# Activation written in turn order, and down weights dealt to partitions to match, in a one-core mixture-of-experts layer

## The chip, the cores and the metric

The kernel runs on one core of one Trainium2 chip. The metric is the device time in microseconds. Before the change it is 1559.59 us, the median of 3 runs (1559.12 to 1560.1).

## The reference, cut to what matters

One layer of a streaming encoder: 512 tokens of width 1024 go through a token mixer (RWKV heads, pooling, forgetting attention), and then through a mixture of 32 experts, of which each token takes its top 4. The change touches only the experts:

```python
def expert_block(args):
    x_blk, e = args                       # 128 tokens of one expert, 1024 wide
    gu = x_blk @ w_gu[e] + b_gu[e]        # w_gu[e]: 1024 x 2048
    gate = jnp.minimum(gu[:, :D_FF], SWIGLU_LIMIT)
    up = jnp.clip(gu[:, D_FF:], -SWIGLU_LIMIT, SWIGLU_LIMIT)
    act = (up + 1.0) * (gate * jax.nn.sigmoid(SWIGLU_ALPHA * gate))
    return act @ w_down[e] + b_down[e]    # w_down[e]: 1024 x 1024, the sum runs over the 1024 columns of act
```

The sum over the columns of `act` may be taken in any order, as long as column f of `act` meets row f of `w_down`.

## The kernel before, in words

**Stages.** The first 320 us or so are the mixer, then come router and output projection, and from about 382 us to 1526 us the experts. One step handles one expert with one block of 128 tokens; there are 32 steps of the same shape, and a few microseconds of combining after them.

**Weights.** Each expert's weights arrive as 12 chunks of 1 MB (128 partitions x 2048 f32): 8 of gate and up (`c < KT`), 4 of down. Each chunk is loaded by SyncE into one of 8 raw slots (`load`, L1602 to L1613), once TensorE has used the chunk 8 before. ScalarE copies it into the rounded form `w_hi` (`split_hi`, L1619; 4 slots, so it waits until TensorE has used the chunk 4 before). VectorE subtracts, `w_lo = w_raw - w_hi` (`split_lo`, L1625), in the raw slot's own place. TensorE multiplies in three parts, 12 matmuls of 512 columns a chunk (`chunk`, L2330), and counts the chunk as used.

**Down chunks before.** Down chunk j holds the rows 256 j to 256 j + 255 of the expert's down weights, two to a partition: partition p has the rows 256 j + 2p and 256 j + 2p + 1. That is 8 KB in one run for a partition, and 1 MB in one run for the chunk.

**The activation.** TensorE leaves gate in PSUM banks 0 and 1 and up (with 1 added by the bias) in banks 2 and 3, as 128 tokens x 1024 columns each. ScalarE writes the sigmoid into `sig_b` (L1776). VectorE makes the product in `act_b` by three instructions in `swiglu(n)`: L2055 (up, clipped, from PSUM), L2058 (times the capped sigmoid, from SBUF), L2061 (times the capped gate, from PSUM). Here all of them read and write columns in their own order, next to each other.

**The turns.** `at_turn(n)` (L2342 to L2348) transposes the activation on TensorE, 128 columns at a time, 8 transposes (L2346) with `act_b` as the operand that is loaded into the array. Turn k = 2j + i takes the columns 256 j + i, + 2, + 4 and so on, so every second column. The transposes of the tokens (`xt`, L2309) have the same shape but read 128 columns next to each other. ScalarE and VectorE split the turned activation into `aTh` (L1763) and `aTl` (L2066, `a_lo`), the tokens into `xTh` and `xTl` (`x_lo`).

**Order on VectorE in step n** (function `step`): `swiglu(n-1)`, `x_lo(n)`, the 8 `split_lo` of gate and up of expert n, `a_lo(n-1)` , the 4 `split_lo` of down of expert n-1. All of it is in program order.

**Order on TensorE in step n**: wait for `swiglu(n-1)`; bias (L2319, 4 matmuls into banks 0 to 3); wait for `xTl`; gate and up chunks 0 to 3; `at_turn(n-1)`; chunks 4 to 7; `xt(n+1)`; the 4 down chunks of expert n-1. Each chunk waits for its `w_lo`.

**Order on ScalarE in step n**: sigmoid of n-1, `xTh`, four `w_hi`, the store of a finished output block, four `w_hi`, `aTh`, four `w_hi`.

In step 1 the `w_lo` of chunk 0 is made before `swiglu(0)` (`EARLY = 1`); in the steps 2 to 31 it is made after `swiglu` and `x_lo`.

Of the kernel before, what the change touches and what calls it, by code (L numbers as in the profile page):

```python
# [20 lines left out]
ALU = mybir.AluOpType  # L21
# [3 lines left out]
P = 128  # L25
D = 1024
S = 512
KT = D // P
# [19 lines left out]
F = 1024  # L48
# [8 lines left out]
CHUNKS = 12  # L57
# [9 lines left out]
LIMIT, ALPHA = 7.0, 1.702  # L67
# [72 lines left out]
def build(nc, a, out):  # L140
    with ExitStack() as ctx:
        def sb(name, shape, dt=F32):
            return ctx.enter_context(nc.sbuf_tensor(name, shape, dt))

        def sem(name):
            return ctx.enter_context(nc.semaphore(name))
# [13 lines left out]
        def Rc(lo, hi):  # L160
            if hi <= LATE:
                return R0[:, lo:hi]
            if hi <= FV_LO:
                return R1[:, lo - LATE:hi - LATE]
            if hi <= FV_HI:
                return R2[:, lo - FV_LO:hi - FV_LO]
            return R1[:, lo - LATE - PZ_LO + FV_LO:hi - LATE - PZ_LO + FV_LO]
        ident = sb("ident", [P, P])
# [30 lines left out]
        sat = sb("sat", [P, 1])  # L199
# [129 lines left out]
        ps = ctx.enter_context(nc.psum_tensor("ps", [P, 8, 512], F32))  # L329
# [104 lines left out]
        up_rdy = sem("up_rdy")  # L434
        half_rdy = sem("half_rdy")
# [11 lines left out]
        act_rdy = sem("act_rdy")  # L447
# [1098 lines left out]
        sig_b, act_b = Rc(11264, 12288), Rc(12288, 13312)  # L1546
# [17 lines left out]
        dn_v = a["moe_w_down"][0].rearrange("e k n -> (e k) n")  # L1564
# [14 lines left out]
        def wait_used(eng, at, back=0):  # L1579

            if len(at) == 3:
                eng.wait_ge(w_used, CHUNKS * at[1] + (CHUNKS * E + at[2] + 1 - back))
            else:
                eng.wait_ge(w_used, 2 * CHUNKS * at[0] + (at[1] + 1 - back))
# [17 lines left out]
        def load(sp, e, c, at, first=False):  # L1602

            if len(at) == 3:
                wait_used(sp, at, 4 if c < RAW_SLOTS else RAW_SLOTS)
            elif not first:
                wait_used(sp, at, RAW_SLOTS)
            s = at[-1] % RAW_SLOTS
            if c < KT:
                src = gu_v[bass.ds(e * D + P * c, P), :]  # L1610
            else:
                src = dn_v[bass.ds(e * F + 2 * P * (c - KT), 2 * P), :].rearrange("(p i) n -> p (i n)", i=2)
            sp.dma_start(w_raw[:, s, :], src).then_inc(raw_in[s], 16)  # L1613

        def split_hi(act, at, first=False):
# [17 lines left out]
        @block.sync  # L1633
        def _(sp):
            sp.wait_ge(rw_out, 2)
            for c in range(KT):
                if c == 2:
                    sp.wait_ge(p_mm, TT)
                load(sp, 0, c, place(0, c), first=True)
            for part in range(3):  # L1640
                sp.dma_start(bdn_all[E * part:E * part + E, :], a["moe_b_down"][0]).then_inc(bdn_in, 16)
            for c in range(CHUNKS):
                load(sp, 1 if c < KT else 0, c, place(1, c))
            sp.wait_ge(ov_rdy, 1)
            sp.dma_start(normfB, a["norm_f"].partition_broadcast(P)).then_inc(normf_in, 16)
            with sp.Fori(1, E // 2) as m:
                for s in range(2):
                    for c in range(CHUNKS):
                        load(sp, 2 * m + s if c < KT else 2 * m + (s - 1), c, lap(m, s, c))
            for c in range(KT, CHUNKS):  # L1650
                load(sp, E - 1, c, place(E, c - KT))
            ov = overflow_count(sp)
            with sp.If(ov > 0):
                sp.wait_ge(flushed, 1)
                with sp.Fori(0, ov) as j:
                    e = sp.value_load(ovI[0:1, bass.ds(j, 1)], min_val=0, max_val=E - 1)
                    for c in range(CHUNKS):
                        load(sp, e, c, extra(j, c))
            for t in range(TT):
                sp.wait_ge(res_rdy, t + 1)  # L1660
                sp.dma_start(out[0, P * t:P * t + P, :], x2[:, t, :]).then_inc(out_done[t % 2], 16)
# [203 lines left out]
        def _(dve):  # L1865
# [14 lines left out]
            v = nc.vector  # L1880

            def two(buf):
                return buf.rearrange("p (b c) -> p b c", b=2)


            dve.wait_ge(small2_in, 16 * SMALL2)
            v.tensor_scalar(braw[HD:P, :, :], braw[HD:P, :, :], 1.0, None, ALU.add).then_inc(bias_one, 1)
# [4 lines left out]
                                   op0=ALU.mult, op1=ALU.add).then_inc(bias_lo, 1)  # L1892
            dve.wait_ge(mod_dma, 16 * 14)
            link(v.scalar_tensor_tensor(out=mod[4], in0=mod[4], scalar=1.0, in1=norm2B,
                                        op0=ALU.add, op1=ALU.mult))
# [61 lines left out]
            for t in range(TT):  # L1957
# [9 lines left out]
                if t == 0:  # L1967
                    mixed_lo(4)
                    for m in (4, 5):
# [6 lines left out]
                                            op0=ALU.mult, op1=ALU.mult))  # L1976
# [75 lines left out]

            def swiglu(n, gu_end):
                wait_used(dve, gu_end)
                v.tensor_scalar(two(act_b), ps[:, 2:4, :], 1.0 - LIMIT, 1.0 + LIMIT, ALU.max, ALU.min).then_inc(up_rdy, 1)  # L2055
                dve.wait_ge(sig_rdy, n + 1)
                dve.wait_ge(up_rdy, n + 1)
                v.scalar_tensor_tensor(out=act_b, in0=sig_b, scalar=sat[:, 0:1], in1=act_b, op0=ALU.min,  # L2058
                                       op1=ALU.mult).then_inc(half_rdy, 1)
                dve.wait_ge(half_rdy, n + 1)  # L2060
                v.scalar_tensor_tensor(out=two(act_b), in0=ps[:, 0:2, :], scalar=LIMIT, in1=two(act_b), op0=ALU.min,  # L2061
                                       op1=ALU.mult).then_inc(act_rdy, 1)

            def turned_lo(n, ev_sem, hi_part, lo_part, lo_sem):
                dve.wait_ge(ev_sem, n + 1)
# [52 lines left out]
            def step(n, where, before, done=0, side=0):  # L2118
                swiglu(n - 1, before(KT - 1))
                x_lo(n)  # L2120
                for c in range(KT):
                    if c >= done:
                        split_lo(dve, where(c))
                    beside(side, c)
                a_lo(n - 1)
                for c in range(KT, CHUNKS):
                    split_lo(dve, where(c))
# [31 lines left out]
            with dve.Fori((TT + 2) // 2, E // 2) as m:  # L2159
                for s in range(2):  # L2160
                    step(2 * m + s, lambda c: lap(m, s, c), lambda c: lap(m, s, c - CHUNKS))
            swiglu(E - 1, place(E - 1, KT - 1))
            split_lo(dve, place(E, 0))
            rows_here(0)
# [11 lines left out]
            with dve.If(ov > 0):  # L2176
                for t in range(1, TT - 1):
                    into_x(t, link_over)
                dve.wait_ge(yg_in[TT - 1], 16 * TOPK)
                link_over(v.tensor_scalar(yg[TT - 1][0], yg[TT - 1][0], gate_of[:, 0, TT - 1, 0:1], None, ALU.mult))  # L2180
                for k in range(1, TOPK):
                    link_over(add_row(TT - 1, 0, k))
                into_x(TT - 1, link_over).then_inc(flushed, 1)
                with dve.Fori(0, ov) as j:
                    x_lo(E + j)
                    for c in range(KT):
                        split_lo(dve, extra(j, c))
                    swiglu(E + j, extra(j, KT - 1))
                    a_lo(E + j)
                    for c in range(KT, CHUNKS):  # L2190
                        split_lo(dve, extra(j, c))

                dve.wait_ge(over_in, 16 * TT * TOPK)
                tail_diag(1, tail_new)
                for t in range(TT - 1):
                    link_over(v.tensor_scalar(yg[t][0], yg[t][0], gate_of[:, 1, t, 0:1], None, ALU.mult))
                    for k in range(1, TOPK):
                        link_over(add_row(t, 1, k))
                link_over(into_x(0, link_over))
# [26 lines left out]
        def _(pe):  # L2226
# [115 lines left out]
            def at_turn(n):  # L2342
                pe.wait_ge(act_rdy, n + 1)
                for k in range(KT):
                    j, i = k // 2, k % 2
                    ins = nc.tensor.transpose(ps[:, 4 + k // 4, P * (k % 4):P * (k % 4) + P],  # L2346
                                              act_b[:, 2 * P * j + i:2 * P * (j + 1):2], ident[:])
                ins.then_inc(at_mm, 1)  # L2348

            def bias_down(t, start):  # L2350
# [68 lines left out]
            step(E - 1, 1, at_step(E - 1), None, E - 2, 1, True)  # L2419
            pe.wait_ge(gmt_rdy, 2)  # L2420
            at_turn(E - 1)
            pe.wait_ge(y_last, 1)
            tail_add(0, 0, True, False)
# [8 lines left out]
            with pe.If(ov > 0):  # L2432
# [3 lines left out]
                with pe.Fori(0, ov) as j:  # L2436
                    n = E + j
# [52 lines left out]
```

## Time and profile before

| | us |
|---|---|
| median of 3 runs | 1559.59 (1559.12 to 1560.1) |
| the profiled execution's own time | 1562.78 |
| its span (first to last instruction) | 1561.0 |
| TensorE busy in the span | 1503.5 |
| VectorE busy | 1375.4 |
| ScalarE busy | 1006.5 |
| GpSimd busy | 225.2 |

The granted TensorE clock is 0.986 of full speed over the span. DMA moves 507.71 MB, 325 GB/s over the span. A matmul's duration in the profile (about 0.39 us for 512 columns) is longer than the distance to the next (about 0.227 us), because matmuls are pipelined; how long work on TensorE takes is read from the distance of starts. "PEld" is the loading of the array, which runs beside the matmuls.

### The profile page before, as it was taken

The page shows a single profiled execution, that of the slowest core. Times are in us where ns is not written, and L with a number is a line of the kernel's source. Part 1 is how long each engine was busy: PE and PEld are TensorE (multiplying, and loading weights), DVE is VectorE, ACT ScalarE, POOL GpSimd, SP SyncE. Part 2 cuts the span into 40 slices and gives each one's busy share as a digit, 9 for nine tenths or more (in the row PEclk, how much of TensorE's full clock was granted, in tenths as well). Part 3 has the DMA queues.
Part 4 walks back from the last instruction along what each step waited for, and adds up shares of the span by engine and source line. Part 5 has one row for each costly group of instructions (what it writes and reads, how often), then busy time and mean ns, then how long its engine had stood idle before and what let it go on. Part 6 is the DMA issues. An engine that isn't in the chain of part 4 may idle for free.

```text
span 1561.0 us, 22569 instructions
## 1 busy us (share of the span) xinstructions
PE 1503.5 (96%) x8449; PEld 1177.0 (75%) x8449; DVE 1375.4 (88%) x1068; ACT 1006.5 (64%) x820; POOL 225.2 (14%) x236
## 2 busy tenths in 40 slices
PE   4999989998899999999999999999999999999996
PEld 2684468666788888888888888888888888888873
DVE  6887577487999999999999999999999999999996
ACT  4332434344577777777777777777777777777762
POOL 3343031000011111111111111111111111110060
PEclk9999999997999999999999999999999999999998
DMA  9679130225899999999999999999999999999992
GB/s 362 259 263 348 58 115 26 73 82 226 299 384 383 390 388 386 379 393 393 395 380 395 384 393 377 384 397 382 384 399 389 381 385 391 384 385 376 378 357 108
DMA packets 89544, 507.71 MB, mean 325 GB/s; under 512 B 11384, under 2 KB 12712, under 8 KB 38160
## 3 DMA queue, kind: packets, MB, share of 16 engines
q1 hardware_dynamic: 74656, 454.65, 74.3%
q0 software_dynamic: 9104, 34.08, 6.3%
q10 hardware_dynamic: 5728, 18.18, 2.9%
q8 instruction: 40, 0.66, 0.2%
q14 instruction: 16, 0.13, 0.0%
HBM read 478.03 MB, written 28.85 MB: 325 GB/s over the span
## 4 chain that ended last, share of the span: by engine, by line
PE 90%; DVE 5%; DMA 2%; ACT 1%; issue 1%; POOL 0%; SPq 0%; DVEq 0%; POOLq 0%; ACTq 0%
PE ps L2330 67%; PE ps L2346 2%; PE ps L1369 2%; PE ps L2309 2%; PE ps L1441 2%; PE ps L1267 2%; PE ps L1355 2%; PE ps L1361 2%; PE ps L1358 2%; DMA Wt<-in_ada_w 1%; PE ps L1363 1%; PE ps L2387 1%; PE ps L2319 1%; PE ps L2236 1%; PE ps L1323 1%
## 5 line engine op out<-in xcount | busy, mean ns | idle before, releaser
L1625 DVE TENSOR_TENSOR w_lo<-w_raw,w_hi 128x2048 fp32r<-128x2048 f32 x384 | 865.2, 2287 | 62.9 <-ACT w_hi L1619 59.5
L1619 ACT ACTIVATE w_hi<-w_raw 128x2048 fp32r<-128x2048 f32 x384 | 736.2, 1919 | 273.2 <-PE ps L2330 273.2
L2330 PE MATMUL ps<-w_hi,xTh 128*128 128x512 f32 x1024 | 407.1, 398 | 2.5 <-DVE xTl L2066 2.2
L2330 PE MATMUL ps<-w_lo,xTh 128*128 128x512 f32 x1024 | 400.5, 391 | 0.0
L2330 PE MATMUL ps<-w_hi,xTl 128*128 128x512 f32 x1024 | 274.7, 390 | 0.0
L2330 PEld LDWEIGHTS ps<-w_hi,xTh 128*128 128x128 f32 x1024 | 193.4, 189 | 49.9 <-issue 7.5
L2330 PEld LDWEIGHTS ps<-w_hi,xTl 128*128 128x128 f32 x1024 | 192.8, 188 | 40.6
L2330 PEld LDWEIGHTS ps<-w_lo,xTh 128*128 128x128 f32 x1024 | 193.3, 189 | 38.1
L2330 PE MATMUL ps<-w_hi,aTh 128*128 128x512 f32 x512 | 202.4, 395 | 0.0
L2330 PE MATMUL ps<-w_lo,aTh 128*128 128x512 f32 x512 | 199.4, 389 | 0.0
L1667 POOL TENSOR_TENSOR carried<-iotaE 128x1 f32<-128x1 f32 x64 | 28.0, 438 | 992.4 <-PE ps L2309 869.7
L2330 PE MATMUL ps<-w_hi,aTl 128*128 128x512 f32 x512 | 157.6, 389 | 0.0
L2330 PEld LDWEIGHTS ps<-w_hi,aTl 128*128 128x128 f32 x512 | 96.1, 188 | 20.1
L2330 PEld LDWEIGHTS ps<-w_lo,aTh 128*128 128x128 f32 x512 | 96.3, 188 | 19.1 <-issue 0.2
L2330 PEld LDWEIGHTS ps<-w_hi,aTh 128*128 128x128 f32 x512 | 96.2, 188 | 19.0 <-issue 0.2
L1679 POOL DMA_INDIRECT xg<-h_rows,icol x30 | 86.4, 2880 | 4.4 <-issue 0.4
L802 ACT ACTIVATE R<-ps,fmx 128x128 f32<-128x128 f32 (+3 forms) x32 | 16.6, 523 | 46.0 <-DVE fmx L1031 46.0
L2058 DVE SCALAR_TENSOR_TENSOR R<-R,sat 128x1024 f32<-128x1024 f32 x32 | 41.1, 1284 | 3.8
L683 POOL TENSOR_TENSOR Wr<-Wt,Wr 128x1024 fp32r<-128x1024 f32 x13 | 35.0, 2695 | 64.7 <-ACT Wr L778 64.7
L2061 DVE SCALAR_TENSOR_TENSOR R<-ps,R 128x1024 f32<-128x1024 f32 x32 | 39.2, 1224 | 1.1
L2055 DVE TENSOR_SCALAR R<-ps 128x1024 f32<-128x1024 f32 x32 | 38.9, 1217 | 0.7 <-PE ps L2330 0.7
L2066 DVE TENSOR_TENSOR xTl<-ps,xTh 128x1024 fp32r<-128x1024 f32 x32 | 38.8, 1213 | 0.6 <-ACT xTh L1763 0.6
(425 smaller groups left out, 1577.1 us busy)
## 6 DMA issues: line engine op xcount, KB each, us to landing
w_raw<-in_moe_w_gu SPq DMA_DIRECT2D x256, 1024.0 KB, 6.9
w_raw<-in_moe_w_down SPq DMA_DIRECT2D x128, 1024.0 KB, 7.7
y_rows<-R ACTq DMA_DIRECT2D x30, 512.0 KB, 7.7
Wt<-in_ada_w SPq DMA_DIRECT2D x10, 1024.0 KB, 4.6
y_rows<-Wt POOLq DMA_DIRECT2D x1, 8704.0 KB, 24.6
Wt<-in_ada_w SPq DMA_DIRECT2D x16, 512.0 KB, 11.7
Wt<-in_w_in SPq DMA_DIRECT2D x4, 2048.0 KB, 9.6
R<-in_ada_w SPq DMA_DIRECT2D x6, 1024.0 KB, 8.2
```

The source lines that it names most:

```text
L683: g.tensor_tensor(blk_lo[at][:, :, c], blk[at][:, :, c], set_hi[i % 2].bitcast(F32), ALU.subtract).then_inc(set_rest, 1)
L1267: ins = mm(job_bank(("rw", m)), blk[0][:, k, P * m:P * m + P], hT[:, k, :], start=(k == 0), stop=(k == KT - 1))
L1355: mm(b, w_hi_[:, k, :], h_hi[:, k, :], start=(k == 0), stop=False)
L1358: mm(b, w_hi_[:, k, :], h_lo[k], start=False, stop=False)
L1619: nc.scalar.activation(w_hi[:, at[-1] % HI_SLOTS, :], w_raw[:, at[-1] % RAW_SLOTS, :], ACT.Copy).then_inc(hi_rdy, 1)
L1625: nc.vector.tensor_tensor(w_lo[:, s, :], w_raw[:, s, :], w_hi[:, at[-1] % HI_SLOTS, :].bitcast(F32), ALU.subtract).then_inc(lo_rdy, 1)
L1679: nc.gpsimd.indirect_dma_start(out=xg[s], out_offset=None, in_=h2_d, in_offset=bass.IndirectOffsetOnAxis(ap=ids, axis=0)).then_inc(xg_in[s ...
L2055: v.tensor_scalar(two(act_b), ps[:, 2:4, :], 1.0 - LIMIT, 1.0 + LIMIT, ALU.max, ALU.min).then_inc(up_rdy, 1)
L2058: v.scalar_tensor_tensor(out=act_b, in0=sig_b, scalar=sat[:, 0:1], in1=act_b, op0=ALU.min, op1=ALU.mult).then_inc(half_rdy, 1)
L2061: v.scalar_tensor_tensor(out=two(act_b), in0=ps[:, 0:2, :], scalar=LIMIT, in1=two(act_b), op0=ALU.min, op1=ALU.mult).then_inc(act_rdy, 1)
L2066: v.tensor_tensor(lo_part[:], ps[:, 4:6, :].rearrange("p b (k t) -> p (b k) t", k=4), hi_part[:].bitcast(F32), ALU.subtract).then_inc(lo_s ...
L2330: ins = mm(ps[:, bank0 + c, :], x[:, k, :], w[:, 512 * (banks * i + c):512 * (banks * i + c) + 512], start=(first and i == 0 and x is xh a ...
```

## The change: what it does

`act_b` is written in the order in which the turns read it: column f = 8 q + k of the product goes to place 128 k + q. `by_k` makes the view in which VectorE's three instructions read their sources: for each k it takes the columns k, k + 8, k + 16 and so on, so consecutive elements lie 8 f32 (32 bytes) apart. `act_k` is the destination and second source, whose elements lie next to each other. Turn k then reads 128 columns next to each other, and holds column 8 q + k in partition q.

To match, the down chunk j has in partition p the rows 8p + 2j and 8p + 2j + 1. A partition still reads 8 KB in one run, but the runs of neighbouring partitions lie 32 KB apart instead of 8 KB.

```diff
             else:
-                src = dn_v[bass.ds(e * F + 2 * P * (c - KT), 2 * P), :].rearrange("(p i) n -> p (i n)", i=2)
+                src = dn_v[bass.ds(e * F, F), :].rearrange("(p c i) n -> p c (i n)", c=CHUNKS - KT, i=2)[:, c - KT, :]
             sp.dma_start(w_raw[:, s, :], src).then_inc(raw_in[s], 16)
...
+            def by_k(banks):
+
+                return banks.rearrange("p b c -> p (b c)").rearrange("p (q k) -> p k q", k=KT)
+
+            act_k = act_b.rearrange("p (k q) -> p k q", k=KT)
...
             def swiglu(n, gu_end):
                 wait_used(dve, gu_end)
-                v.tensor_scalar(two(act_b), ps[:, 2:4, :], 1.0 - LIMIT, 1.0 + LIMIT, ALU.max, ALU.min).then_inc(up_rdy, 1)
+                v.tensor_scalar(act_k, by_k(ps[:, 2:4, :]), 1.0 - LIMIT, 1.0 + LIMIT, ALU.max, ALU.min).then_inc(up_rdy, 1)
                 dve.wait_ge(sig_rdy, n + 1)
                 dve.wait_ge(up_rdy, n + 1)
-                v.scalar_tensor_tensor(out=act_b, in0=sig_b, scalar=sat[:, 0:1], in1=act_b, op0=ALU.min,
-                                       op1=ALU.mult).then_inc(half_rdy, 1)
+                v.scalar_tensor_tensor(out=act_k, in0=by_k(two(sig_b)), scalar=sat[:, 0:1], in1=act_k,
+                                       op0=ALU.min, op1=ALU.mult).then_inc(half_rdy, 1)
                 dve.wait_ge(half_rdy, n + 1)
-                v.scalar_tensor_tensor(out=two(act_b), in0=ps[:, 0:2, :], scalar=LIMIT, in1=two(act_b), op0=ALU.min,
-                                       op1=ALU.mult).then_inc(act_rdy, 1)
+                v.scalar_tensor_tensor(out=act_k, in0=by_k(ps[:, 0:2, :]), scalar=LIMIT, in1=act_k,
+                                       op0=ALU.min, op1=ALU.mult).then_inc(act_rdy, 1)
...
                 for k in range(KT):
-                    j, i = k // 2, k % 2
                     ins = nc.tensor.transpose(ps[:, 4 + k // 4, P * (k % 4):P * (k % 4) + P],
-                                              act_b[:, 2 * P * j + i:2 * P * (j + 1):2], ident[:])
+                                              act_b[:, P * k:P * k + P], ident[:])
                 ins.then_inc(at_mm, 1)
```

## Rows read from the trace of the kernel before

**Rows 1.** The page: busy time by engine.

```profile
PE 1503.5 (96%) x8449; PEld 1177.0 (75%) x8449; DVE 1375.4 (88%) x1068; ACT 1006.5 (64%) x820; POOL 225.2 (14%) x236
```

**Rows 2.** The page: lines in the chain that ended last, share of span.

```profile
PE ps L2330 67%; PE ps L2346 2%; PE ps L1369 2%; PE ps L2309 2%; PE ps L1441 2%; PE ps L1267 2%; PE ps L1355 2%; PE ps L1361 2%; PE ps L1358 2%; DMA Wt<-in_ada_w 1%; PE ps L1363 1%; PE ps L2387 1%; PE ps L2319 1%; PE ps L2236 1%; PE ps L1323 1%
```

**Rows 3.** Waits, whole span: engine, line, waited for: us total, times, longest.

```profile
ACT w_hi L1619 <- PE ps L2330: 273.2, 343, 6.0
DVE w_lo L1625 <- ACT w_hi L1619: 59.5, 150, 0.5
```

**Rows 4.** Windows, one step: length, busy by engine, PEclk, DMA share, GB/s.

```profile
600.00:635.18 35.18, 35.18 (x166) 28.94 (x165) 32.87 (x18) 26.68 (x18) 3.95 (x4) 1.00 0.99 389
```

**Rows 5.** Timeline, VectorE, one step: start us, us, instruction.

```profile
1009.10 1.22 DVE L2055 TENSOR_SCALAR R<-ps 128x1024 f32<-128x1024 f32 x1
1010.44 1.28 DVE L2058 SCALAR_TENSOR_TENSOR R<-R,sat 128x1024 f32<-128x1024 f32 x1
...
1014.03 15.73 DVE L1625 TENSOR_TENSOR w_lo<-w_raw,w_hi 128x2048 fp32r<-128x2048 f32 x7
```

**Rows 6.** Timeline, TensorE, the same step: start us, us, instruction.

```profile
1003.83 1.07 PE L2330 MATMUL ps<-w_hi,xTl 128*128 128x512 f32 x4
...
1005.53 0.48 PE L2330 MATMUL ps<-w_hi,aTh 128*128 128x512 f32 x1
...
1017.03 0.51 PE L2330 MATMUL ps<-w_hi,xTh 128*128 128x512 f32 x1
...
1019.87 0.39 PE L2330 MATMUL ps<-w_hi,xTh 128*128 128x512 f32 x1
...
1027.12 1.08 PE L2330 MATMUL ps<-w_hi,xTl 128*128 128x512 f32 x4
...
1028.91 0.48 PE L2330 MATMUL ps<-w_hi,xTh 128*128 128x512 f32 x1
```

**Rows 7.** Groups by form, array loads of the turns: busy us, mean ns, idle.

```profile
L2346 PEld LDWEIGHTS ps<-ident,R 128*128 128x128 f32 x256 | 35.7, 207 | 2.4
L2309 PEld LDWEIGHTS ps<-ident,xg 128*128 128x128 f32 x256 | 29.7, 140 | 6.2 <-DMA xg<-h_rows,tok 2.2
```

**Rows 8.** Groups by form, VectorE: busy us, mean ns, idle before.

```profile
L1907 DVE TENSOR_REDUCE R<-R 128x32 bf16<-128x128 f32 x4 | 1.5, 371 | 0.1
L1933 DVE TENSOR_REDUCE R<-R 128x4 f32<-128x128 f32 x1 | 0.3, 286 | 0.0
...
L1057 DVE SCALAR_TENSOR_TENSOR R<-R,cols 128x512 f32<-128x512 f32 x6 | 10.6, 1773 | 0.2
L1057 DVE SCALAR_TENSOR_TENSOR Wt<-Wt,cols,R 128x512 f32<-128x512 f32 x2 | 1.5, 752 | 0.1
```

**Rows 9.** Timeline, TensorE, start of step 1; the bracket is the idle before.

```profile
416.39 0.50 PE L2319 MATMUL ps<-bparts,sel 32*128 32x512 f32 x4 [3.17 <-DVE R L2061]
```

**Rows 10.** Windows around two idle times of TensorE; PEclk is third last.

```profile
416.00:418.00 2.00, 0.98 (x5) 0.67 (x6) 2.00 (x3) 2.00 (x3) 0.00 (x0) 0.80 0.88 328
418.00:420.00 2.00, 2.00 (x6) 1.52 (x6) 2.00 (x2) 1.81 (x2) 0.00 (x0) 0.50 0.32 127
420.00:422.00 2.00, 2.00 (x9) 1.61 (x8) 2.00 (x2) 0.00 (x0) 0.00 (x0) 0.85 0.00 0
...
1530.00:1532.00 2.00, 1.88 (x3) 0.85 (x4) 0.48 (x1) 0.00 (x0) 0.00 (x0) 0.50 0.05 10
```

**Rows 11.** Timeline, TensorE, in the tail.

```profile
1530.12 7.01 PE L2387 MATMUL ps<-gap,R 128*128 128x512 f32 x12 [2.02 <-issue]
```

**Rows 12.** The page: DMA issues, KB each, median us to landing.

```profile
w_raw<-in_moe_w_down SPq DMA_DIRECT2D x128, 1024.0 KB, 7.7
...
Wt<-in_ada_w SPq DMA_DIRECT2D x10, 1024.0 KB, 4.6
...
Wt<-in_w_out SPq DMA_DIRECT2D x2, 1024.0 KB, 4.9
```

**Rows 13.** Windows: the part of a step with the fastest transfers.

```profile
1017.00:1039.00 22.00, 22.00 (x104) 18.34 (x101) 20.62 (x10) 16.58 (x10) 0.00 (x0) 1.00 1.00 406
```

## The prediction, made before the changed kernel was built or run

> **What bounds the kernel now.** I read the busy times first: TensorE is busy 96% of the span and VectorE 88% [rows 1]. The chain of waits says which of them counts: 67% of the span is the expert matmuls of L2330, and VectorE's split does not appear among its lines [rows 2]. The waits agree: ScalarE waits 273.2 us for TensorE to free a `w_hi` slot, and VectorE waits for ScalarE 150 times, never over 0.5 us [rows 3]. So TensorE sets the pace and all others follow it. But they follow closely. One step lasts 35.18 us; TensorE fills it, VectorE is busy 32.87 us of it, and DMA has a share of 0.99 at 389 GB/s [rows 4]. VectorE has 2.3 us a step to spare in all. What it has to spare at its tightest place is less, and that decides this change.
>
> That place is the start of a step. VectorE runs its three swiglu instructions from 1009.10 on and `x_lo` after them, and only then can it make `w_lo` of gate/up chunk 0, which starts at 1014.03 [rows 5]. A lone split takes 2.29 us (seven back to back take 15.73, so 2.24 from start to start), so chunk 0 is ready at 1016.32. TensorE starts that chunk at 1017.03 [rows 6]. The cover is 1017.03 - 1016.32 = 0.71 us. For chunk 1 it is larger: ready at 1018.56, used at 1019.87, so 1.3 us, and it grows by some 0.5 us a chunk, since a chunk lasts 2.72 us on TensorE and 2.24 on VectorE. Hence: if swiglu grows by g, every step from 2 to 31 (30 steps) loses g - 0.71 where g is over 0.71, and nothing below it. VectorE's spare time doesn't soften this: its start at 1009.10 follows from when TensorE freed slots, and the step gets longer by the stall, so it always catches up before the next swiglu (idle 2.3 - 0.7 = 1.6 us a step for any g).
>
> **The turns (gain).** The 8 turns of the activation read every second column, the 8 of the tokens read neighbouring ones; all else is equal. An array load takes 207 ns in the first and 140 ns in the second [rows 7]. Most of that is hidden behind matmuls; the path shows how much isn't. From the start of the last group of four matmuls before the turns to the first matmul after them it is 1005.53 - 1003.83 = 1.70 us for the tokens and 1028.91 - 1027.12 = 1.79 us for the activation [rows 6]. The change makes the second like the first: 0.09 us a step, 32 steps, 2.9 us. Bounds: 0 below, and 8 x 67 ns x 32 = 17 us above if the loads were all exposed, which the distances speak against. I take 2.9.
>
> **The three VectorE instructions (cost).** They keep their number, size and destination order, but one source of each is now read at 32 bytes from element to element: PSUM in L2055 and L2061, SBUF in L2058. The trace has one VectorE row with a source at a wide step: the reduce of L1907 reads its 128 f32 at 128 bytes each and takes 371 ns; the same operation over as many neighbouring f32, L1933, takes 286 ns [rows 8]. That is 85 ns / 128 = 0.66 ns an element, so 1024 x 0.66 = 0.68 us for an instruction. For PSUM at a step no row exists. Below, the bound is 0 for each (nothing about a stride can make a read faster than one in order, and the path to PSUM might not mind it). Above, the farthest row in which the same operation on the same shape goes slower is L1057, 1773 ns against 752 for 512 elements [rows 8], 2.0 ns an element or 2.04 us for each. I take the 0.68 of the only strided row for all three: g = 2.04 us. The ends are g = 0 and g = 6.1.
>
> What it costs: stall 2.04 - 0.71 = 1.33 us in 30 steps, 40.0 us. In step 1 TensorE already waits 3.17 us for L2061 of `swiglu(0)` with nothing to cover it [rows 9], so there g counts in full: 2.0 us. At the end nothing is added for g up to 3: `at_turn(31)` comes behind four down chunks, where the other steps have their bias. The other waits that move by g have more cover than chunk 0. `xTl` is ready at about 1014.1 [rows 5], 2.9 us before 1017.03. The activation is made one `x_lo` (1.2 us) earlier, at 1012.9, and the bias, half a microsecond long [rows 9], starts at about 1016.5, so its cover is 3.6 us.
>
> The Vector Engine (DVE) Microarchitecture Reference of the Trainium skill, section Measured stream behaviour on trn2, says that a port keeps full rate only for runs of at least two adjacent 4-byte words, and gives 1.73 ns an element against 1.054 where one source hops 4 KiB every element. The row of L1907 agrees (0.66 ns more). The same table gives 2.50 for short steps of 24 words on both sources; by that price, as an estimate, g would be 3 x 1.48 = 4.4 us and the sum 1673 us. No row here tells which of the two an 8-word step is.
>
> **The down weights (taken at nothing).** As many DMAs, as many bytes, 8 KB runs as before, only 32 KB apart. The work that hides them is the same wait for TensorE. The nearest rows: 1 MB of `ada_w` in 8 KB runs that lie 192 KB apart lands 4.6 us after issue, 1 MB of `w_out`, one contiguous block, 4.9 us [rows 12]. So a wide distance costs nothing there. I take 0; the other end is in the rivals.
>
> **Sum.** 1562.78 (the profiled execution's own time) - 2.9 + 40.0 + 2.0 = 1601.9 us. That execution is 3.19 us above the median of the runs; set against the median the same sum is 1559.6 + 39.1 = 1598.7 us, and this is the forecast: slower by 2.5%. With g between 1.4 and 2.6 (PSUM a bit cheaper or dearer than SBUF) it is 1579 to 1616.
>
> **Rivals.**
> B, *the read from PSUM does not mind the step.* Then g is 0.68 (only L2058) or 0. The first is just covered by the 0.71: -2.9 + 0.7 = -2.2, 1557.4 us; the second gives 1556.7 us. This is the other side: not slower. It turns at g = 0.71 + about 0.1. For it speaks that PSUM is another memory than the one the strided row reads; against it that L2055 and L2061 run at the same pace as reads from SBUF, so one engine port may set both.
> C, *the stall lowers TensorE's clock.* After the idle 3.17 us of step 1 the granted clock was 0.80, 0.50 and 0.85 in three windows of 2 us [rows 10], a loss of 1.7 us over the wait itself; after an idle time of 2.02 us in the tail it was 0.50 as well [rows 10, 11]. If a stall of 1.3 us did this each step: 30 x 1.7 = 51, 1650 us. Against it: both rows have longer idle times than 1.3 us.
> D, *an 8-word step is dearer.* With twice the addition of L1907, g = 4.1, the stall 3.4: 30 x 3.4 + 4.1 - 2.9 = 103, 1662 us, and 1713 with C's loss, which would then be likely. With the upper bound g = 6.1 it is 30 x 5.4 + 6.1 - 2.9 = 165, 1725 us. VectorE has no row at 8 words, so the profile can't exclude it.
> E, *the down transfers get slower.* A step moves 389 x 35.18 = 13.7 MB, of it 4.2 MB of down. The best stretch reached 406 GB/s [rows 13]: 9.5 MB take 23.4 us at it, which leaves 11.8 us for the down chunks. It decides once they run under 356 GB/s, 12% below. At 25% less a step takes 37.1 us: 31 x 1.9 = 60, 1619 us. Rows 12 speak against it. The page DMA: Bandwidth & Descriptors of the Trainium skill, section Latency and other measured facts, reports 207 GB/s for rows 512 KiB apart and 103 for 4 MiB; at that price the kernel would be far above my range, but the distance here is a sixteenth of the smallest in that list, and no run here shows such a pitch.
>
> **How the numbers follow.** A 0.47, B 0.24, C 0.12, D 0.13, E 0.04. A change smaller than 0.2% (3.1 us) can't be told from none. B's two values are gains of 2.2 and 2.9 us, within that, so most of B counts as same and only a little more gain at the turns makes it faster: faster 0.07, same 0.17; the rest, 0.76, is slower. The range must reach down to B, 1556.5, and up past C and the first value of D, 1668. The likeliest case's own range is 1579 to 1616.
>
> **What would show it.** The turns: array loads of L2346 at 140 ns, and 1.70 us across them. The cost: L2055, L2058 and L2061 at about 1.90, 1.96 and 1.90 us; the seven splits after them start 2.0 us later against `swiglu`'s start; the first matmul of chunk 0 waits for `w_lo` L1625 by 1.3 us in each of 30 steps, a releaser that in the waits before is nearly absent; the step is 36.4 us. For B the two PSUM instructions keep 1.22 us. For C the granted clock in a step falls below 1.00. For D the three take 2.6 us or more. For E ScalarE's `w_hi` waits for DMA in the down chunks, and the landing of the down loads goes from 7.7 us past 10. The forecast is wrong if the three instructions add up to less than 1 us or more than 3 us, or if TensorE's wait lies anywhere but at chunk 0.

## The result, and the profile after

The changed kernel takes 1569.05 us (median of 6 runs, 1565.91 to 1571.52), the kernel before, run beside it, 1559.84 us (1558.14 to 1561.65). The ratio is 1.0054 with a 95% interval from 1.0043 to 1.0066: slower by 8.4 us by the ratio, by 9.2 us by the two medians. The forecast was slower by 39 us. The direction was right, the size off by a factor of more than four. The time lies below the likeliest case's own range (1579 to 1616), and inside the whole range (1556.5 to 1668) only because that reaches down to rival B. The profiled execution took 1570.89 us, its span is 1569.1 us.

The three VectorE instructions, by form (busy us, mean ns, idle before), and the array loads of the turns, against [rows 7]:

```profile
L2063 DVE SCALAR_TENSOR_TENSOR R<-R,sat 128x1024 f32<-128x1024 f32 x32 | 70.6, 2207 | 3.8
L2066 DVE SCALAR_TENSOR_TENSOR R<-ps,R 128x1024 f32<-128x1024 f32 x32 | 39.2, 1225 | 1.1
L2060 DVE TENSOR_SCALAR R<-ps 128x1024 f32<-128x1024 f32 x32 | 39.0, 1218 | 0.9 <-PE ps L2335 0.9
...
L2350 PEld LDWEIGHTS ps<-ident,R 128*128 128x128 f32 x256 | 29.8, 140 | 4.1
```

This decides it. The two instructions that read PSUM at 32 bytes a step take 1218 and 1225 ns, as in order (L2055 had 1.22 us, [rows 5]). The one that reads SBUF takes 2207 ns instead of 1.28 us [rows 5], 0.90 ns an element more. So g, the time by which swiglu gets longer, is 0.93 us, not 2.04. The loads of the turns are at 140 ns, as forecast.

VectorE's timeline in one step (start us, us, instruction), against [rows 5]:

```profile
1015.35 1.22 DVE L2060 TENSOR_SCALAR R<-ps 128x1024 f32<-128x1024 f32 x1
1016.69 2.21 DVE L2063 SCALAR_TENSOR_TENSOR R<-R,sat 128x1024 f32<-128x1024 f32 x1
1018.93 1.23 DVE L2066 SCALAR_TENSOR_TENSOR R<-ps,R 128x1024 f32<-128x1024 f32 x1
1020.08 1.22 DVE L2071 TENSOR_TENSOR xTl<-ps,xTh 128x1024 fp32r<-128x1024 f32 x1
1021.21 17.88 DVE L1625 TENSOR_TENSOR w_lo<-w_raw,w_hi 128x2048 fp32r<-128x2048 f32 x8
```

From swiglu's start to the first split it is 5.86 us, before it was 1014.03 - 1009.10 = 4.93: the same 0.93. TensorE in the same and the next step, against [rows 6]; the bracket is the idle time before an instruction and its releaser:

```profile
1022.85 0.51 PE L2324 MATMUL ps<-bparts,sel 32*128 32x512 f32 x4
1023.55 0.49 PE L2335 MATMUL ps<-w_hi,xTh 128*128 128x512 f32 x1 [0.20 <-DVE w_lo L1625]
...
1033.67 1.07 PE L2335 MATMUL ps<-w_hi,xTl 128*128 128x512 f32 x4
1034.58 1.03 PE L2350 MATMUL ps<-ident,R 128*128 128x128 f32 x8
1035.37 0.48 PE L2335 MATMUL ps<-w_hi,xTh 128*128 128x512 f32 x1
...
1058.24 0.50 PE L2324 MATMUL ps<-bparts,sel 32*128 32x512 f32 x4
```

The wait lies where the prediction put it, at `w_lo` of chunk 0, and a step is 1058.24 - 1022.85 = 35.39 us instead of 35.18 (35.36 to 35.41 in the steps 5 to 29; the steps 2 to 4 take 35.45 to 35.53, the step 30 35.47). Across the turns it is 1035.37 - 1033.67 = 1.70 us, where it was 1.79. The wait is now there once in each of 30 steps, where the kernel before had it once, 0.2 us long (engine, line, waited for: us, times, longest), against [rows 3]:

```profile
DVE w_lo L1625 <- ACT w_hi L1619: 43.1, 117, 0.4
PE ps L2335 <- DVE w_lo L1625: 6.2, 30, 0.4
PEld ps L2335 <- DVE w_lo L1625: 13.1, 26, 0.6
```

and the chain of the page passes through it, against [rows 2]:

```profile
PE ps L2335 45%; DVE w_lo L1625 7%; DVE R L2063 4%; ACT w_hi L1619 4%; DVE xTl L2071 2%; DVE R L2060 2%; PE ps L1369 2%; PE ps L1441 2%; PE ps L2350 2%; PE ps L1267 2%; PE ps L1355 2%; PE ps L1361 2%; PE ps L1358 2%; DMA Wt<-in_ada_w 1%; PE ps L1363 1%
```

Step 1 waits for swiglu(0) with no cover, against [rows 9]: 3.96 us instead of 3.17.

```profile
418.83 0.80 PE L2324 MATMUL ps<-bparts,sel 32*128 32x512 f32 x4 [3.96 <-DVE R L2066]
```

By these rows one would sum 30 x 0.20 + 0.8 = 6.8 us. From the bias of the first step to that of the last it is in fact 7.6 us more (1097.9 against 1090.3 us), since the steps 2 to 4 lose up to 0.35 us each. The spans of the two profiled executions differ by 8.1 us: the changed one also reaches its first expert 1.4 us later, which this change doesn't touch, and regains 0.9 us behind the bias of the last step.

### The profile page after: what moved, and what is told of

It is laid out like the page before. It is cut to its first block, busy times and chain, and to the rows that moved or that the text cites. A ratio compares the mean times of both kernels' runs of the same rounds, so it can differ in the third digit from the quotient of the medians.

```text
span 1569.1 us, 22569 instructions
## 1 busy us (share of the span) xinstructions
PE 1504.3 (96%) x8449; PEld 1174.2 (75%) x8449; DVE 1400.8 (89%) x1068; ACT 1006.1 (64%) x820; POOL 227.7 (15%) x236
## 4 chain that ended last, share of the span: by engine, by line
PE 64%; DVE 22%; ACT 5%; issue 5%; DMA 3%; POOL 1%; DVEq 0%; SPq 0%; ACTq 0%; POOLq 0%
PE ps L2335 45%; DVE w_lo L1625 7%; DVE R L2063 4%; ACT w_hi L1619 4%; DVE xTl L2071 2%; DVE R L2060 2%; PE ps L1369 2%; PE ps L1441 2%; PE ps L2350 2%; PE ps L1267 2%; PE ps L1355 2%; PE ps L1361 2%; PE ps L1358 2%; DMA Wt<-in_ada_w 1%; PE ps L1363 1%
## 5 line engine op out<-in xcount | busy, mean ns | idle before, releaser
L2335 PEld LDWEIGHTS ps<-w_hi,xTl 128*128 128x128 f32 x1024 | 193.0, 189 | 41.1
L2335 PEld LDWEIGHTS ps<-w_lo,xTh 128*128 128x128 f32 x1024 | 193.7, 189 | 38.6
L2063 DVE SCALAR_TENSOR_TENSOR R<-R,sat 128x1024 f32<-128x1024 f32 x32 | 70.6, 2207 | 3.8
L2071 DVE TENSOR_TENSOR xTl<-ps,xTh 128x1024 fp32r<-128x1024 f32 x32 | 38.9, 1215 | 2.2 <-ACT xTh L1763 2.2
L2066 DVE SCALAR_TENSOR_TENSOR R<-ps,R 128x1024 f32<-128x1024 f32 x32 | 39.2, 1225 | 1.1
L2060 DVE TENSOR_SCALAR R<-ps 128x1024 f32<-128x1024 f32 x32 | 39.0, 1218 | 0.9 <-PE ps L2335 0.9
```

The lines of the kernel that those rows point to most:

```text
L2060: v.tensor_scalar(act_k, by_k(ps[:, 2:4, :]), 1.0 - LIMIT, 1.0 + LIMIT, ALU.max, ALU.min).then_inc(up_rdy, 1)
L2063: v.scalar_tensor_tensor(out=act_k, in0=by_k(two(sig_b)), scalar=sat[:, 0:1], in1=act_k, op0=ALU.min, op1=ALU.mult).then_inc(half_rdy, 1)
L2066: v.scalar_tensor_tensor(out=act_k, in0=by_k(ps[:, 0:2, :]), scalar=LIMIT, in1=act_k, op0=ALU.min, op1=ALU.mult).then_inc(act_rdy, 1)
L2071: v.tensor_tensor(lo_part[:], ps[:, 4:6, :].rearrange("p b (k t) -> p (b k) t", k=4), hi_part[:].bitcast(F32), ALU.subtract).then_inc(lo_s ...
L2335: ins = mm(ps[:, bank0 + c, :], x[:, k, :], w[:, 512 * (banks * i + c):512 * (banks * i + c) + 512], start=(first and i == 0 and x is xh a ...
```

## The experiments

Theory: a step loses g - c, where g is what swiglu grows by and c the cover at chunk 0, and gains 0.08 at the turns; only the read from SBUF makes g. Rivals: the down rows cost a part; PSUM order or the clock has a hidden share; the loss isn't a stall with a threshold. Each run was timed beside the kernel before. Step lengths come from the starts of the bias matmuls of two successive steps.

**The turns alone.**

```diff
-                                              act_b[:, 2 * P * j + i:2 * P * (j + 1):2], ident[:])
+                                              act_b[:, P * k:P * k + P], ident[:])
```

> Part changed alone: the turns read 128 neighbouring columns of the activation; activation order and down rows stay as before (so columns of the activation meet other rows of the down weights; the work is the same). Theory A (the turns are on the path, worth what the change's own trace shows): array loads of the turns 140 ns instead of 207, a step of 35.09 us instead of 35.18, 32 x 0.09 = 2.9 us less, 1556.9 us. Rival B (the loads are hidden, the step was shortened by nothing): a step of 35.18, same time within 0.1%.

Measured: 1558.18 against 1560.45 us, ratio 0.9984 (0.9974 to 0.9993), loads of 140 ns, and a step of 35.10 us:

```profile
1017.64 0.50 PE L2319 MATMUL ps<-bparts,sel 32*128 32x512 f32 x4
...
1052.74 0.50 PE L2319 MATMUL ps<-bparts,sel 32*128 32x512 f32 x4
```

The gain is real, 0.08 us a step, 2.5 us in all. Rival B falls.

**The read from SBUF alone.**

```diff
-                v.scalar_tensor_tensor(out=act_b, in0=sig_b, scalar=sat[:, 0:1], in1=act_b, op0=ALU.min,
+                act_k = act_b.rearrange("p (k q) -> p k q", k=KT)
+                v.scalar_tensor_tensor(out=act_k, in0=by_k(two(sig_b)), scalar=sat[:, 0:1], in1=act_k, op0=ALU.min,
                                        op1=ALU.mult).then_inc(half_rdy, 1)
```

> Part changed alone: the middle of VectorE's three instructions reads the sigmoid from SBUF at 32 bytes from element to element; both reads from PSUM, the turns and the down rows stay as before (the sigmoid meets other columns than its own; the work is the same). Theory A (this one read is the whole loss): that instruction 2.21 us instead of 1.28, the cover at chunk 0 is 0.64 us, so TensorE loses 0.93 - 0.64 = 0.29 us in each of 30 steps, a step of 35.47 us, and 0.9 us in step 1: 1559.8 + 8.7 + 0.9 = 1569.4 us, as slow as the whole change or slightly slower. Rival B (the down rows cost part of the loss): the step stays under 35.38 us and the time under 1566 us.

Measured: 1570.16 us, ratio 1.0056 (1.0043 to 1.0069), +8.7 us by the ratio; the instruction, the wait at chunk 0 and the length of a step as theory A had them (35.47 us in the step shown, 35.45 in the mean of the steps 5 to 30):

```profile
L2063 DVE SCALAR_TENSOR_TENSOR R<-R,sat 128x1024 f32<-128x1024 f32 x32 | 70.6, 2206 | 3.8
...
PEld ps L2335 <- DVE w_lo L1625: 15.8, 28, 2.3
...
1023.91 0.50 PE L2324 MATMUL ps<-bparts,sel 32*128 32x512 f32 x4
...
1059.38 0.50 PE L2324 MATMUL ps<-bparts,sel 32*128 32x512 f32 x4
```

This one operand is the whole loss.

**The down rows alone.**

```diff
-                src = dn_v[bass.ds(e * F + 2 * P * (c - KT), 2 * P), :].rearrange("(p i) n -> p (i n)", i=2)
+                src = dn_v[bass.ds(e * F, F), :].rearrange("(p c i) n -> p c (i n)", c=CHUNKS - KT, i=2)[:, c - KT, :]
```

> Part changed alone: the down weights' rows lie 32 KB apart from partition to partition; activation and turns stay as before (so columns of the activation meet other rows of the down weights; the work is the same). Theory A (rows of 8 KB move equally fast wherever they lie): a step of 35.18 us, the down loads land within 0.5 us of 7.7 after issue, same time within 0.1%. Rival B (the far rows load the DMA engines more): down loads land over 1 us later, the step gets longer by 0.1 to 0.2 us, +3 to +6 us.

Measured: ratio 0.9998 (0.9988 to 1.0008), a step of 1054.55 - 1019.37 = 35.18 us, and the down loads land 7.4 us after issue, where [rows 12] had 7.7 (issues, KB each, median us to landing):

```profile
w_raw<-in_moe_w_down SPq DMA_DIRECT2D x128, 1024.0 KB, 7.4
```

Rows 32 KB apart cost nothing. Rival B of this run and rival E of the prediction fall.

**The change without the strided SBUF read.** ScalarE reads gate from PSUM in the turns' order and writes the sigmoid so, and VectorE's middle instruction reads neighbours. The edit is against the changed kernel.

```diff
-                s_.activation(sig_b.rearrange("p (b c) -> p b c", b=2), ps[:, 0:2, :], ACT.Sigmoid, scale=ALPHA
+                s_.activation(sig_b.rearrange("p (k q) -> p k q", k=KT),
+                              ps[:, 0:2, :].rearrange("p b c -> p (b c)").rearrange("p (q k) -> p k q", k=KT),
+                              ACT.Sigmoid, scale=ALPHA
...
-                v.scalar_tensor_tensor(out=act_k, in0=by_k(two(sig_b)), scalar=sat[:, 0:1], in1=act_k,
+                v.scalar_tensor_tensor(out=act_b, in0=sig_b, scalar=sat[:, 0:1], in1=act_b,
```

> The changed kernel, but ScalarE already writes the sigmoid in turn order (it reads gate from PSUM at 32 bytes from element to element and writes neighbours), so VectorE's middle instruction reads neighbours; the two reads from PSUM by VectorE keep their step. Nothing is left out. Theory A (the loss is the strided read from SBUF alone, and PSUM does not mind the step for ScalarE either): the middle instruction back at 1.28 us, the sigmoid at 1.0 us, no stall at chunk 0, a step of 35.09 us, only the gain of the turns left: 1556.9 us, faster than both kernels. Rival B (VectorE's order of reading PSUM or the order of the down rows has a hidden cost that the durations don't show): a step over 35.2 us and a time over 1561 us. Rival C (ScalarE's read from PSUM at a step costs 0.9 us): the sigmoid 1.9 us, VectorE starts its middle instruction 0.6 us later and 1560 to 1562 us.

Measured: 1558.15 against 1560.45 us, ratio 0.9983 (0.9972 to 0.9994), a step of 35.10 us. The middle instruction is back at 1285 ns, and the sigmoid, read at a step from PSUM, takes 1007 ns, where it took 1006 before:

```profile
L2065 DVE SCALAR_TENSOR_TENSOR R<-R,sat 128x1024 f32<-128x1024 f32 x32 | 41.1, 1285 | 3.8
...
L1776 ACT ACTIVATE R<-ps 128x1024 f32<-128x1024 f32 x32 | 32.2, 1007 | 2.3 <-PE ps L2337 2.3
...
1018.29 0.50 PE L2326 MATMUL ps<-bparts,sel 32*128 32x512 f32 x4
...
1053.39 0.50 PE L2326 MATMUL ps<-bparts,sel 32*128 32x512 f32 x4
```

It is faster than both kernels: all of the change's gain, none of its cost. Rivals B and C fall.

**The law of the cover.** Three kernels lengthen the swiglu of the kernel before by reduces that the layer doesn't need; n and w are 1 and 420, 2 and 920, 4 and 920. Their sums go to `spare`, in SBUF columns that also hold `tailG`, which the combining at the end reads. So the sums are read, though the expectation below says that nobody reads them, and these kernels' output is not the layer's. The work beside the reduces is that of the kernel before.

```diff
                                        op1=ALU.mult).then_inc(half_rdy, 1)
+                for i in range(n if made[0] < 8 else 0):
+                    v.tensor_reduce(spare[:, i:i + 1], sig_b[:, 0:w], AX_X, ALU.add)
```

> The kernel before, with one more VectorE instruction between the second and third of swiglu: a reduce over 420 columns of the sigmoid, whose result nobody reads, in steps 1 to 31. It makes swiglu longer by g = 0.45 us. Theory A (the law: a step loses g minus a cover of about 0.65 us at chunk 0, nothing below it): g is inside the cover, the step stays 35.18 us, only step 1 is longer by 0.45; the time within 0.1% of before. Rival B (VectorE's time counts in part at any size): the step grows by some share of 0.45, at half of it +7 us.

> The same with two such reduces over 920 columns: g = 2.0 us, the amount that the prediction had assumed for the strided reads. Theory A (law with a cover of 0.65): stall 1.35 us, step 36.5 us, and with 2.0 us in step 1 the time is 1560.4 + 40.5 + 2 = 1603 us; the granted clock stays at full speed in the steps. Rival B (a stall of this size lowers TensorE's clock in each step, the prediction's rival C): step 38.2 us, 1653 us, granted clock under 1.00. Rival C (the real cover is VectorE's idle time of a whole step, 2.3 us, and the small stall of the change came from elsewhere): step 35.2 us.

> The same with four such reduces: g = 4.1 us, the amount of the prediction's rival D. Theory A (the law goes on with slope 1): stall 3.4 us, step 38.6 us, 1560.4 + 103 + 4 = 1667 us. Rival B (after a stall over 2 us the clock falls, as it did in step 1 and in the tail): step 40.3 us, 1718 us, granted clock 0.95 or less over the steps. Rival C (VectorE becomes the bound, busy 32.9 + 4.1 = 37.0 us): step 37.0 us, 1618 us.

g is read as the time from swiglu's first start to the first split, minus 4.93.

| | g | step | stall (step - 35.18) | cover (g - stall) | ratio to before (95%) |
|---|---|---|---|---|---|
| one reduce | 0.37 | 35.18 | 0 | - | 1.0006 (0.9993 to 1.0019) |
| SBUF read alone | 0.93 | 35.45 | 0.27 | 0.66 | 1.0056 (1.0043 to 1.0069) |
| two reduces | 1.91 | 36.44 | 1.26 | 0.65 | 1.0252 (1.023 to 1.0274) |
| mixed patterns (below), steps at full clock | 2.94 | 37.49 | 2.31 | 0.63 | not compared |
| four reduces | 3.94 | about 38.5, 40.1 or 41.1, in no fixed order | 3.3 in the shortest | 0.64 | 1.0932 (1.0908 to 1.0955) |

The step lengths are means over the steps 5 to 30 (7 to 30 for the mixed patterns), for four reduces the values that occur. VectorE and TensorE around one step of the kernel with two reduces:

```profile
1029.98 1.22 DVE L2059 TENSOR_SCALAR R<-ps 128x1024 f32<-128x1024 f32 x1
1031.32 1.29 DVE L2062 SCALAR_TENSOR_TENSOR R<-R,sat 128x1024 f32<-128x1024 f32 x1
1032.52 2.12 DVE L2065 TENSOR_REDUCE R<-R 128x1 f32<-128x920 f32 x2
1034.56 1.22 DVE L2067 SCALAR_TENSOR_TENSOR R<-ps,R 128x1024 f32<-128x1024 f32 x1
...
1036.82 17.88 DVE L1625 TENSOR_TENSOR w_lo<-w_raw,w_hi 128x2048 fp32r<-128x2048 f32 x8
...
1039.15 0.50 PE L2336 MATMUL ps<-w_hi,xTh 128*128 128x512 f32 x1 [1.17 <-DVE w_lo L1625]
```

The law holds in all five: nothing below the cover, slope 1 above, cover 0.63 to 0.66 us, though VectorE had 2.3 us idle a step in the kernel before. Two reduces have nearly the g that the prediction had assumed. They take 1600.25 us, 39.3 more than the kernel before; the prediction's sum for g = 2.04 without the gain of the turns is 42.0, the law with g = 1.91 gives 30 x 1.26 + 1.9 = 39.7. Rival B of one reduce and rivals B and C of two fall.

With four reduces (1707.08 us) the law alone gives 30 x 3.3 + 4 = 103, and 146 us were lost. The rest is the clock, as rival B had it (1718 us); rival C's 1618 is out. After one of TensorE's stalls of 2.75 us it was granted half speed (1.2 GHz) for some microseconds (windows: length, busy by engine, PEclk, DMA share, GB/s):

```profile
1060.99 0.80 PE L2336 MATMUL ps<-w_hi,xTh 128*128 128x512 f32 x1 [2.75 <-DVE w_lo L1625]
...
1060.00:1065.00 5.00, 4.01 (x10) 3.18 (x11) 5.00 (x3) 0.21 (x1) 0.00 (x0) 0.50 0.75 310
1065.00:1070.00 5.00, 5.00 (x21) 4.07 (x20) 4.07 (x3) 2.64 (x2) 0.00 (x0) 0.86 0.42 139
1070.00:1075.00 5.00, 5.00 (x26) 4.22 (x25) 4.11 (x3) 3.40 (x3) 0.00 (x0) 1.00 0.98 385
```

Not every such stall does this. In the steps 2 to 30 of this kernel all stalls at chunk 0 are 2.74 to 2.92 us long; behind 8 of them the clock stayed full for the whole step (38.5 to 38.9 us), 12 steps had a mean clock of 0.96 (40.1 to 40.2 us) and 9 of 0.92 (40.9 to 41.3 us). The kernel with mixed patterns has stalls of 2.1 to 2.3 us in its steps 6 to 30, and the clock fell in 2 of these 25. One stall of each kind, and one step of each length (windows as above):

```profile
781.26 0.50 PE L2336 MATMUL ps<-w_hi,xTh 128*128 128x512 f32 x1 [2.75 <-DVE w_lo L1625]
778.00:816.47 38.47, 35.34 (x164) 28.94 (x164) 36.77 (x22) 26.51 (x18) 3.95 (x4) 1.00 0.90 352
816.47:856.69 40.22, 36.95 (x164) 30.07 (x164) 37.05 (x22) 26.79 (x18) 3.95 (x4) 0.96 0.88 340
1057.70:1098.82 41.12, 37.85 (x164) 30.81 (x164) 37.05 (x22) 26.79 (x18) 3.96 (x4) 0.92 0.86 334
...
596.08 0.80 PE L2344 MATMUL ps<-w_hi,xTh 128*128 128x512 f32 x1 [2.17 <-DVE w_lo L1625]
```

With the 1.2 us of two reduces the clock stayed at 1.00 in all steps from 2 on (2.4 GHz). So rival C of the prediction was no danger at the stall that it had in view, and is one in most steps at twice that. What decides which stall of the same length brings the clock down stays open. With four reduces g also passes the second cover that the prediction gave, 3.6 us at the bias: TensorE waits 0.4 to 0.7 us there in each step, but the wait at chunk 0 ends later and alone sets the loss.

**Which reads at a step cost.**

```diff
+                K = (2, 4, 16, 32, 128, 8, 8, 64, 64)[f]
+                hop = lambda m: m.rearrange("p (q k) -> p k q", k=K)
+                near = lambda m: m.rearrange("p (k q) -> p k q", k=K)
...
+                v.scalar_tensor_tensor(out=dst, in0=src(sig_b), scalar=sat[:, 0:1], in1=one, op0=ALU.min,
+                                       op1=ALU.mult).then_inc(half_rdy, 1)
```

> The kernel before, but each step's three swiglu instructions read and write in another pattern (the columns then meet other columns; the work is the same, so only the durations of these instructions are read, not the total). Sources at a step of 2, 4, 16, 32, 128 elements in steps 1 to 5; from step 6 on, in turn, source next to each other with destination and second source at a step of 8, and all three at a step of 8. Theory A (a read from SBUF is at full rate only where two 4-byte neighbours are read together, and the step beyond that doesn't matter; PSUM does not mind): the middle instruction 2.2 us at every step from 2 on, the two with PSUM sources 1.22 us. Rival B (what counts is the distance in bytes): at a step of 2 and 4 under 1.6 us, and from 8 on 2.2 us. Rival C (the larger the step the cheaper, as 0.66 ns an element at a step of 32 in L1907 against 0.90 at 8 in the change): 1.95 us at a step of 32 and 128. For a strided write: 1.22 us if writes don't mind, 2.1 us or more if they do.

From step 6 on, destination and second source have the step of 8 in both patterns, and the first source is in turn in order and at a step of 8. A strided second source with a destination in order was not run, so for L2072 and L2075 the price of the second source and that of the write can't be told apart; L2069 has one source, so its 2.12 us are the write's. The steps 4, 16, 32 and 128 have one instance each, in a single run. VectorE's timeline (L2069 and L2075 have PSUM as first source, L2072 has SBUF):

```profile
411.81 1.28 DVE L2072 SCALAR_TENSOR_TENSOR R<-R,sat 128x1024 f32<-128x1024 f32 x1
...
445.58 2.11 DVE L2072 SCALAR_TENSOR_TENSOR R<-R,sat 128x1024 f32<-128x1024 f32 x1
447.73 1.22 DVE L2075 SCALAR_TENSOR_TENSOR R<-ps,R 128x1024 f32<-128x1024 f32 x1
...
550.58 1.22 DVE L2069 TENSOR_SCALAR R<-ps 128x1024 f32<-128x1024 f32 x1
551.91 2.11 DVE L2072 SCALAR_TENSOR_TENSOR R<-R,sat 128x1024 f32<-128x1024 f32 x1
...
585.91 2.12 DVE L2069 TENSOR_SCALAR R<-ps 128x1024 f32<-128x1024 f32 x1
588.15 2.32 DVE L2072 SCALAR_TENSOR_TENSOR R<-R,sat 128x1024 f32<-128x1024 f32 x1
...
627.15 2.39 DVE L2072 SCALAR_TENSOR_TENSOR R<-R,sat 128x1024 f32<-128x1024 f32 x1
```

From SBUF a step of 2 elements is free (1.28 us), from 4 on the price is there and hardly moves: 2.11, 2.05, 2.16 and 2.11 us at 4, 16, 32 and 128, and 2.21 at 8 in the change. From PSUM no step costs anything (1.22 us throughout). A write to SBUF at a step of 8 costs the same kind of price (2.12 us for L2069, with its source in order). The prices hardly add up: with all three operands at a step of 8 the middle instruction takes 2.39 us. So none of the expectations alone is right: the distance matters between 8 and 16 bytes and not beyond.

**Turn order at TensorE instead.** The down rows of the change, the activation in its own order, the turns reading every eighth column.

```diff
-                                              act_b[:, 2 * P * j + i:2 * P * (j + 1):2], ident[:])
+                                              act_b[:, k:D:KT], ident[:])
```

> The order of the change made at the other end: VectorE writes the activation in its own order as before, the down rows are dealt as in the change, and turn k reads every eighth column (32 bytes from element to element) as the operand that TensorE loads. Nothing is left out. Theory A (a load pays for leaving neighbours once, as VectorE's read does, so a step of 8 is like the step of 2 of before): loads of 207 ns, a step of 35.18 us, the time of before within 0.1%. Rival B (a load pays by distance): loads of 280 ns or more, the turns 0.1 to 0.6 us longer a step, +3 to +18 us.

Measured: 1558.34 against 1560.37 us, ratio 0.9991 (0.9982 to 1.0), loads of 191 ns, a step of 35.12 us:

```profile
L2345 PEld LDWEIGHTS ps<-ident,R 128*128 128x128 f32 x256 | 33.6, 191 | 2.7
...
1014.98 0.50 PE L2319 MATMUL ps<-bparts,sel 32*128 32x512 f32 x4
...
1050.10 0.50 PE L2319 MATMUL ps<-bparts,sel 32*128 32x512 f32 x4
```

For the loads both expectations missed: a load at a step of 8 is cheaper than one at a step of 2 (207 ns [rows 7]), not as dear or dearer. Why isn't settled. The time is within 0.1% of before, as theory A had it; the steps are 0.06 us shorter, read from the trace.

**The gain without the cost, within VectorE.** Reads at a step of 2, even columns first, then odd ones; the down rows as in the kernel before.

```diff
+            def by_pair(flat):
+
+                return flat.rearrange("p (q i) -> p i q", i=2)
+
+            act_k = act_b.rearrange("p (i q) -> p i q", i=2)
...
+                v.scalar_tensor_tensor(out=act_k, in0=by_pair(sig_b), scalar=sat[:, 0:1], in1=act_k, op0=ALU.min,
...
-                                              act_b[:, 2 * P * j + i:2 * P * (j + 1):2], ident[:])
+                                              act_b[:, 4 * P * i + P * j:4 * P * i + P * (j + 1)], ident[:])
```

> The gain without the cost: VectorE reads its three sources at a step of 2 elements (8 bytes) and writes the even columns, then the odd ones, next to each other; each turn then reads 128 neighbours, and the down rows stay as in the kernel before. Nothing is left out. Theory A (a step of 2 from SBUF is free, as step 1 of the run with mixed patterns showed with 1.28 us for the middle instruction): 1.28 us in all 32 steps, loads of the turns 140 ns, a step of 35.10 us, ratio to before 0.998, about 1558 us, level with the version in which ScalarE writes the sigmoid in turn order. Rival B (that one row was an accident of step 1, where TensorE and DMA were quiet): the middle instruction near 2.1 us, a step of 35.37 us, about 1569 us.

Measured: 1558.6 us, ratio 0.9991 (0.9982 to 1.0001); the middle instruction 1284 ns in all 32 steps, loads of 140 ns, a step of 1048.78 - 1013.68 = 35.10 us:

```profile
L2065 DVE SCALAR_TENSOR_TENSOR R<-R,sat 128x1024 f32<-128x1024 f32 x32 | 41.1, 1284 | 3.8
```

In the steps it equals the version with ScalarE. Its whole-kernel ratio alone doesn't clear the noise; that the steps are shorter by 0.08 us is read from the trace.

## Why the prediction missed, point by point

- **What bounds the kernel, and where the cover lies**: right. TensorE's new wait is at `w_lo` of chunk 0 and at no other chunk, and the cover is 0.63 to 0.66 us, forecast 0.71. The difference is about the hand-over: the forecast counted from the end of the split to the start of the first matmul as if the signal took no time. In the changed kernel it takes 0.05 us (the split starts at 1021.21 and takes 2.29, the matmul starts at 1023.55).
- **The turns**: right, forecast 0.09 us a step, measured 0.08; 2.5 us instead of 2.9.
- **The three VectorE instructions**: this is the step that failed, as a size: "I take the 0.68 of the only strided row for all three: g = 2.04 us". Two of the three terms, the reads from PSUM, are 0 instead of 0.68, the lower bound that the prediction itself had set. The third, from SBUF, is 0.93 instead of 0.68: L1907 [rows 8] jumps at every element too, but its price an element was 0.66 ns against 0.90. It is another operation (a reduce of 128 elements), and it differs from L1933 in more than the step: it writes 32 bf16 sums, L1933 four f32. How much of its 85 ns is the step's is not shown. So g was 0.93 instead of 2.04, and as the cover is subtracted, the stall fell from 1.33 to 0.29 us: halving g took away more than three quarters of the loss. The prediction had named three instructions adding up to less than 1 us as a sign that it is wrong, and they add up to 0.93.
- **Step 1**: right in kind, g counts in full: 0.8 us, as in this one swiglu the middle instruction takes 2.07 us and not 2.21.
- **The down rows**: right, taken at nothing, and nothing they cost.
- **Rivals.** B had the mechanism (PSUM does not mind the step) but a price for SBUF just within the cover; at 0.93 it is outside it, so the kernel got slower all the same. That the direction came out right is part luck: the stall of 1.33 us behind it was not there, and with B's own price for SBUF the kernel would have come out level. I had given B 0.24 and no case the outcome between B and the forecast, though a third more on B's one term is enough to reach it. C and D did not happen; the runs with reduces show what they would have been (D with C's loss was put at 1713 us, 153 over before, and four reduces cost 146). E is excluded.
- **The page on VectorE streams** (Vector Engine (DVE) Microarchitecture Reference of the Trainium skill, section Measured stream behaviour on trn2) wants runs of at least two adjacent words. The free step of 2 elements (1.28 us, no two words of a read adjacent) does not fit that as it is put; the measurement decides. Its 1.73 ns an element for one source that hops 4 KiB and its 2.50 for both sources at a step of 24 words lie on either side of 1.95 ns, an estimate for one source at 8 words: the page's 1.05 ns in order and the 0.90 measured here.

## What to carry to other kernels

An engine's idle time over a stage is not its cover: VectorE had 2.3 us a step to spare, but 0.65 us at the one place where TensorE waits for it, and only the second number counts. Look which memory each operand of a strided instruction lies in before pricing it, and price reads from PSUM and from SBUF apart. If an order must be made, let the instruction that reads PSUM make it (here ScalarE's sigmoid), or keep the step at 2 elements.

## What the runs showed of the hardware that was not expected

- VectorE and ScalarE read f32 from PSUM at a step of 8 elements as fast as in order (VectorE 1218 and 1225 ns, ScalarE 1007 ns, for 128x1024), VectorE at every step from 2 to 128.
- VectorE reads f32 from SBUF at a step of 2 elements at full rate (1.28 us for 1024) and at 4 to 128 elements in 2.05 to 2.24 us. A write to SBUF at a step of 8 brings a 1.22 us instruction to 2.12 us.
- TensorE's array load of 128x128 f32 takes 140 ns from neighbours, 207 ns at a step of 2 and 191 ns at a step of 8.
- Stalls of 1.2 us once in 36 us left TensorE's clock at full speed; stalls of 2.1 to 2.3 us once in 37.5 us brought it to half speed for some microseconds in 2 of 25 steps, stalls of 2.75 to 2.9 us once in 38.5 to 41 us in 21 of 29, where the step was 1.5 to 2.7 us longer than the mean of those at full clock (38.6 us).
